# The last quarter of a down projection with tokens as rows, its earlier sum turned by VectorE

## The reference

```python
def conv_ffn(x, prev, up, cw, cb, down):
    a = x @ up
    gate, val = jnp.split(a, 2, axis=-1)
    gc, new = causal_conv(gate, prev, cw)
    h = jax.nn.gelu(gc + cb, approximate=True) * val
    return h @ down, new
...
    f, new_ffn = conv_ffn(rmsnorm(x, g_ffn_pre), ffn_prev, ffn_up, ffn_conv_w, ffn_conv_b, ffn_down)
    x = x + rmsnorm(f, g_ffn_post)
```

## Time and profile before

| | |
|---|---|
| median of three runs | 1332.47 us (1332.05 to 1333.07) |
| the profiled execution: its own time | 1332.47 us |
| the profiled execution: span from first to last instruction | 1330.8 us |
| mean granted TensorE clock | 0.999 |
| busy share of the span: PE, PEld, DVE, ACT, POOL | 99%, 99%, 60%, 38%, 5% |
| mean DMA rate | 150 GB/s |

### The profile page before, as it was taken

One profiled execution on the slowest core, in us unless ns is written; L12 is line 12 of the kernel. 1 busy time (PEld: TensorE's weight loads), 2 busy tenths in 40 slices (PEclk: granted clock), 3 DMA queues, 4 the chain that ended last, 5 costly groups with the idle time before them and its releaser, 6 DMA issues.

```text
span 1330.8 us, 24552 instructions
## 1 busy us (share of the span) xinstructions
PE 1319.8 (99%) x8970; PEld 1312.0 (99%) x8970; DVE 798.7 (60%) x1256; ACT 500.6 (38%) x726; POOL 73.2 (5%) x186
## 2 busy tenths in 40 slices
PE   9999999999999999999999999999999999999997
PEld 8999999999999999999999999999999999999996
DVE  7758755544488655556655544555555455655875
ACT  7323333234464333323333332333333333333552
POOL 0051000000041000000000000000000000000000
PEclk9999999999999999999999999999999999999999
DMA  9754455565554554556455455645544565555453
GB/s 245 199 158 128 133 147 138 157 160 139 155 134 134 152 157 128 140 148 183 133 152 156 131 137 152 180 138 153 150 137 131 152 180 145 151 146 138 131 145 129
DMA packets 378792, 199.61 MB, mean 150 GB/s; under 512 B 4216, under 2 KB 375588, under 8 KB 378748
## 3 DMA queue, kind: packets, MB, share of 16 engines
q1 hardware_dynamic: 377940, 198.16, 54.2%
q10 hardware_dynamic: 736, 0.66, 0.2%
q0 software_dynamic: 80, 0.31, 0.1%
HBM read 195.68 MB, written 3.56 MB: 150 GB/s over the span
## 4 chain that ended last, share of the span: by engine, by line
PE 98%; DVE 1%; DMA 0%; issue 0%; SPq 0%; ACT 0%; DVEq 0%; ACTq 0%
PE mm L552 31%; PE mm L556 31%; PE mm L553 31%; DVE y_rows L1807 1%; PE tb L811 1%; PE tb L552 1%; PE tb L815 1%; PE tb L556 1%; PE tb L812 1%; PE tb L553 1%; PE tb L642 0%; DMA x_tok<-in_x_sample_dram 0%; PE tb L856 0%; PE tb L731 0%; PE mm L900 0%; PE mm L901 0%
## 5 line engine op out<-in xcount | busy, mean ns | idle before, releaser
L552 PE MATMUL mm<-a_hi,w_hi 128*128 128x320 f32 x1856 | 577.1, 311 | 0.2
L556 PE MATMUL mm<-a_lo,w_hi 128*128 128x320 f32 x1856 | 573.6, 309 | 0.0
L553 PE MATMUL mm<-a_hi,w_lo 128*128 128x320 f32 x1856 | 573.6, 309 | 0.0
L960 ACT ACTIVATE w_hi<-raw 128x1024 fp32r (+3 forms) x378 | 346.8, 965 | 441.7 <-PE mm L556 431.4
L1289 DVE TENSOR_TENSOR w_lo<-raw,w_hi 128x1024 fp32r<-128x1024 f32 (+1 forms) x376 | 409.5, 1130 | 112.9 <-ACT w_hi L960 112.2
L552 PEld LDWEIGHTS mm<-a_hi,w_hi 128*128 128x128 f32 x1856 | 348.5, 188 | 1.6 <-DVE w_lo L1330 0.5
L553 PEld LDWEIGHTS mm<-a_hi,w_lo 128*128 128x128 f32 x1856 | 348.5, 188 | 0.3
L556 PEld LDWEIGHTS mm<-a_lo,w_hi 128*128 128x128 f32 x1856 | 348.4, 188 | 0.0
L556 PE MATMUL mm<-m_lo,w_hi 128*128 128x320 f32 x884 | 273.2, 309 | 0.0
L552 PE MATMUL mm<-h_hi,w_hi 128*128 128x320 f32 x660 | 204.6, 310 | 0.0
L553 PE MATMUL mm<-h_hi,w_lo 128*128 128x320 f32 x660 | 204.0, 309 | 0.0
(11 more groups left out here) (277 smaller groups left out, 938.0 us busy)
## 6 DMA issues: line engine op xcount, KB each, us to landing
raw<-in_ffn_up_dram SPq DMA_DIRECT2D x88, 1024.0 KB, 5.8
raw<-in_ffn_down_dram SPq DMA_DIRECT2D x60, 704.0 KB, 4.8
raw<-in_w_in_dram SPq DMA_DIRECT2D x31, 1024.0 KB, 5.7
raw<-in_w_out_dram SPq DMA_DIRECT2D x16, 1024.0 KB, 6.0
raw<-in_ffn_down_dram SPq DMA_DIRECT2D x2, 1024.0 KB, 5.1
raw<-in_w_in_dram SPq DMA_DIRECT2D x3, 512.0 KB, 10.5
out_dram<-y_rows SPq DMA_DIRECT2D x6, 256.0 KB
x_tok<-in_x_prompt_dram SPq DMA_DIRECT2D x5, 256.0 KB, 4.3
```

The costliest lines, as they stand in the source:

```text
L552: pe.matmul(out, whi[:, s], hi, start=start, stop=False)
L553: pe.matmul(out, wlo[:, s], hi, start=False, stop=False)
L556: return pe.matmul(out, whi[:, s], tile(lo, k), start=False, stop=stop)
L960: act.activation(w_hi[:, d:d + half], src, ACT.Copy).then_inc(w_hi_done, 1)
```

## The change

The down projection of the last group is made wholly with tokens as rows: four blocks of 512 columns, each in the three PIECES, so 12 steps s = 0 to 11 in place of 12 chunks and three pieces. In each step of the first three blocks the order is tile 0, tile 1, tile 2; in the last block it is as before (tiles 2 and 0 through all three pieces, then tile 1). There are four sets of banks (`ROW_BANKS`), and `BANK_FREE` says which step waits for which bank. The first three blocks start in empty banks, and VectorE adds the sum of the first three groups afterwards (`add_rows`). That sum, 12 blocks of `f`, is turned by VectorE in blocks of 32x32 (`turn_f`): for tiles 0 and 1 it is written to the six `tb` banks during the last group's up steps, three instructions after each step, and ScalarE copies the six banks to `f_tok` when the up projection is over; for the samples eight instructions write to SBUF (`f_s`). ScalarE squares rows and sums them along the row (`square_block`), VectorE multiplies by the gain (`gain_block`), which is now loaded as a whole (128x2048) to the place of `f`. The transposes of `turn_unit` for f, `token_sums(4)`, the addition of blocks, their squares and their sum in `acc` are gone. The transposes of the states (seven), of the last block's earlier sum (eight, `seed_rows`) and of the samples' (four) stay.

```diff
+        ROW_BANKS = [(mm[0], mm[1], tb[0]), (tb[3], tb[1], tb[4]), (tb[2], tb[5], mm[0]), (mm[1], tb[3], tb[0])]
+        F_BANKS = [(b, i) for b in range(QD - 1) for i in range(2)]
...
+                if s == 4:
+                    sp.wait_ge(f_blocks, N_F_BLOCKS + 8)
+                    sp.dma_start(gain[:, :], g_ffn_post.to_broadcast([P, D])).then_inc(gain_b_in, 16)
...
+            BANK_FREE = {(0, 0): (drained[0], c_rows // 2), (0, 1): (drained[1], c_rows // 2),
+                         (0, 2): (taken, len(F_BANKS)), (2, 0): (taken, len(F_BANKS) + 2), (2, 2): (rows_added, 1),
+                         (3, 2): (rows_added, 3)}
+            for s in range(3 * QD - 3):
+                b, j = s // 3, s % 3
+                pe.wait_ge(w_lo_done, 2 * (c_rows + s) + 2)
+                if b == 0:
+                    pe.wait_ge(h_hi_done, h0 + sum(PIECES[j]))
+                    pe.wait_ge(h_lo_done, h0 + sum(PIECES[j]))
+                for i in range(3):
+                    if j == 0 and (b, i) in BANK_FREE:
+                        pe.wait_ge(*BANK_FREE[b, i])
+                    last = rows(i, s)
+                    if i == 2:
+                        last.then_inc(used, 1)
+                    elif j == 2:
+                        last.then_inc(rows_done, 1)
+                    if i == 0:
+                        if s in (4, 5):
+                            turn_ffn_states(s - 4)
+                        if s == 7:
+                            turn_samples()
+                        if s == 8:
+                            seed_rows(0)
+                            seed_rows(1)
+            pe.wait_ge(*BANK_FREE[3, 2])
+            for s in range(3 * QD - 3, 3 * QD):
+                pe.wait_ge(w_lo_done, 2 * (c_rows + s) + 2)
+                last = rows(2, s)
...
                 act.preload_act_table(ACT.Sqrt)
-                for m in range(WIDE):
...
+                act.wait_ge(f_blocks, N_F_BLOCKS)
+                act.wait_ge(used, c_rows)
+                for b, i in F_BANKS:
+                    act.activation(f_tok[3 * b + i][:, :], tb[3 * i + b][:, :], ACT.Copy).then_inc(taken, 1)
+                act.wait_ge(ssq_zeroed, 1)
+                for s in range(1, 3 * QD - 2):
+                    split_wide(s + 1)
+                    if s == 3 * QD - 3:
+                        split_wide(s + 2)
+                    if s in (4, 5):
+                        take_states(s - 4)
+                    if s % 3 == 0:
+                        copy_lows(s // 3 - 1)
+                        square_block(s // 3 - 1)
...
+            def turn_f(i, b, a):
+
+                t0 = TT[i][0] + 32 * b
+                dst = f_s[32 * b:32 * b + 32, :] if i == 2 else \
+                    tbs[32 * b:32 * b + 32, (QD - 1) * 512 * i:(QD - 1) * 512 * (i + 1)]
+                dve.transpose(dst.rearrange("p (k c) -> p k c", c=P)[:, :, 32 * a:32 * a + 32],
+                              f[32 * a:32 * a + 32, 0:WIDE * T].rearrange("p (k t) -> p k t", t=T)[:, :, t0:t0 + 32]
+                              ).then_inc(f_blocks, 1)
+
+            def last_up_steps():
+                g = GROUPS - 1
+                f_todo = [(i, b, a) for i in range(2) for b in range(4) for a in range(4)]
+                for i in range(NG):
+                    up_step(g, i, g * NG + i,
+                            blocks=[4 * nk for _, nk in PIECES[0:2]] if i == NG - 1 else (KD, KD))
+                    for block in f_todo[3 * i:3 * i + 3]:
+                        turn_f(*block)
...
+                dve.wait_ge(used, c_rows)
+                for b in range(2):
+                    for a in range(4):
+                        turn_f(2, b, a)
+                dve.wait_ge(f_blocks, N_F_BLOCKS + 8)
+                dve.wait_ge(taken, len(F_BANKS))
+                for s in range(1, 3 * QD - 1):
+                    if s < 3 * QD - 2:
+                        split_wide(s + 1)
+                    if s == 3 * QD - 3:
+                        split_wide(s + 2)
+                    if s % 3 == 0:
+                        add_rows(s // 3 - 1)
+                    if s == 4:
+                        dve.wait_ge(gain_b_in, 16)
+                    if s % 3 == 1 and s > 3:
+                        gain_block(s // 3 - 1)
+                    for block in BLOCKS[EARLY_BLOCKS + PER_CHUNK * (s - 1):EARLY_BLOCKS + PER_CHUNK * s]:
+                        turn_block(*block)
```

More of the change, by code:

```diff
@@ L176, in hybrid_layer @@
     assert at["ws"] + D * 4 <= at["conv_hist"]
[L177 to L188, removed]
+    c_rows = 2 * (C_FFN // 2 + (GROUPS - 1) * (PER_GROUP // 2) + NG)
+    f_s = sb("f_s", [P, (QD - 1) * 512], where="a_hi", plus=28672)
+    f_tok = [f_s[:, n // 3 * 512:(n // 3 + 1) * 512] if n % 3 == 2 else
+             sb(f"f_tok{n}", [P, 512], where="a_hi", plus=16384 + 2048 * (n // 3 * 2 + n % 3))
+             for n in range(3 * (QD - 1))]
+    f_tok += [sb("f_last0", [P, 512], where="a_hi", plus=34816),
+              sb("f_last1", [P, 512], where="a_hi", plus=36864),
+              sb("f_last2", [P, 512], where="f", plus=D * 4 + 2048)]
+    junk = sb("junk", [P, 512], where="a_hi", plus=38912)
+    gain = sb("gain", [P, D], where="f")
+    s_low = sb("s_low", [TS, 512], where="f", plus=D * 4)
+    ssq = sb("ssq", [P, 3 * QD], where="conv_hist")
+    rest = sb("rest", [P, 4], where="conv_hist", plus=64)
+    most = sb("most", [P, 4], where="conv_hist", plus=96)
     wx_hi = sb("wx_hi", [P, 4 * 512], F32R, where="xT")
@@ L495, in load_group @@
                     load(q, 1, wcols(up, NF + g * NG + i))
[L496 to L501, removed]
+                if n_pairs:
+                    with sp.Fori(0, n_pairs) as i:
+                        q = C_FFN // 2 + g * (PER_GROUP // 2) + NG + i
+                        for e in range(2):
+                            rows = down[:, g * NG:(g + 1) * NG] if type(g) is int else \
+                                down[:, bass.ds(g * NG, NG)]
+                            load(q, e, rows[:, :, bass.ds((2 * i + e) * P, P)], NG)
             load_group(0, KD // 2, 3)
@@ L925, in _ @@
-                if j == 1:
-                    pe.wait_ge(drained[1], q_end)
-                    token_sums(4)
-            for j in range(len(PIECES)):
-                last = rows(1, j)
+            for s in range(3 * QD - 3, 3 * QD):
+                last = rows(1, s)
             last.then_inc(rows_done, 1)
@@ L1156, in up_step @@
                 if not early:
[L1157 removed]
+                    split_hi(q + 1, 1, blocks[1])
             def up_steps(g, i0=0):
@@ L1161, in up_steps @@
                     up_step(g, i, g * NG + i)
-                up_step(g, NG - 1, g * NG + NG - 1, blocks=NG)
+                up_step(g, NG - 1, g * NG + NG - 1,
+                        blocks=[4 * nk for _, nk in PIECES[0:2]] if type(g) is int and g == GROUPS - 1 else (NG, NG))
             def group(g, last):
```

257 lines of the change are left out of this document (112 added, 145 removed).

## The result

The changed kernel takes 1335.99 us in the median (1333.84 to 1337.58, 13 executions), the kernel before in the same comparison 1332.57 us (1332.03 to 1333.99, 13 executions): a ratio of 1.0021, with a 95% interval of 1.0013 to 1.0028. It is slower by about 0.2%, 2.2 us over the 1333.8 that was predicted and 0.2 us inside the upper end of the range. That it lies inside the range is luck: the range reached up there for late weights, which did not come, and was meant to leave out the clock, whose own range began at 1335.5 us. The scatter is the first thing to notice: 3.7 us between executions, where before had 2.0.

A forecast was written before the change was run, and what follows sets the result against it. TensorE, busy 99% of the span, was taken to bound the kernel. A saving of 2.28 us, a 3.1 us wait and 0.47 us of VectorE lateness gave +1.3 on 1332.47: 1333.8 us, range 1330.5 to 1336.2.

The forecast's parts named there:

- late weights: Slower rival in the last group's steps: VectorE's splits or a load come late; two us of waits give 1335.8; chance 0.12.
- the clock: Slower rival at the seam: TensorE's clock falls to half in the gap, giving 1335.5 to 1340.6 us; chance 0.08.
- TensorE's work: Last group, until the samples are done: 72.37 us in place of 74.65, a saving of 2.28 us (1.51 to 2.89).
- The seam: After the up projection, tile 2 of step 0 waits for ScalarE's six copies: TensorE stands still 3.1 us (2.8 to 3.6).
- The steps: Down projection steps of 7.3 or 5.5 us run without a wait for weights; closest is step 2, 2 us to spare.
- the third rival: Weights late, slower: additions, gains and turns delay VectorE's splits, or the 1 MB gain holds up a load; chance 0.12.
- The end: Ahead of `f_last`, VectorE's splits, additions, gains and small sums make it 0.47 us late (0 to 1.1).
- The sum: Whole kernel: -2.28 + 3.1 + 0.47 = +1.3, giving 1333.8 us, bounds 1332.4 to 1335.3; chance 0.62.
- the row: Clock windows at the run's end: granted clock falls to half 4.6 us after TensorE's end, so 3.1 us pass unpunished.
- the prediction's own signs of being wrong: VectorE's PSUM writes far over 0.7 us, the clock row leaving 1.00 behind the seam, or weights waited for.

The follow-up runs named there:

- c: The change with tile 0's three banks copied first, each tile's copies waiting only for its own 16 turns, tile 2 for its own bank's copy: 1330.30 us, ratio 0.9984.
- b: The change, but tile 2 of step 0 waits only for the copy freeing its own bank, block 1's tile 0 for the sixth: 1330.96 us, ratio 0.9986.
- f_best: c with the samples' third of the last gain moved on VectorE behind the second half of `f_last`: 1329.91 us, ratio 0.9984 to the kernel before.
- d_filled: The change with thirteen products with zeros as weights ahead of the seam's wait, so TensorE works through the hole: 1333.32 us, ratio 1.0005.
- a_same: The changed kernel again, nothing edited, for a second profiled execution: 1334.67 us, ratio 1.0016 to the kernel before.
- e: The change with three more ScalarE copies into an unread buffer ahead of the six, for a longer hole: 1337.10 us, ratio 1.0037.
- h: The same kernel as c, unchanged, run again beside f_best on the same chip: 1330.09 us, ratio 0.9984 to the kernel before.

## Why the prediction was right in its sum and missed the median

- **TensorE's work**: predicted 72.37 us, measured 72.63 (run c). With the 2.07 for the transposes that is 0.2298 for each of the 307 products in place of 0.229; the saving is 2.02, not 2.28. Right within its bounds.
- **The seam**: predicted 3.1 us, the row says 3.15, and it costs 75.74 (1313.73 - 1237.99) - 72.63 = 3.11. The steps were right too: VectorE ends `m_lo` 2.38 us after the seam (2.37), splits for 1.83 (1.82), turns twice in 1.23 (1.14: a turn to PSUM is 0.62 there, between the bounds), and ScalarE copies for 3.04 (3.0). That it is this wait, and not the turns themselves, that costs is shown by b and c: with it shorter or gone the change gains 0.14 to 0.16%.
- **The steps**: no wait of TensorE for weights in any profile. Right, and with it the third rival falls.
- **The end**: predicted 0.47 us of lateness. `f_last` starts 1.05 us after the samples are done, 0.98 before, and 0.90 in f_best, where nothing stands ahead of it: VectorE is 0.15 late, which puts +0.07 in the sum. Right in kind and too large, since the three gains were done (1314.28) when the copy of `s_low` ended (1314.53), and only the small sums were not.
- **The sum**: -2.02 + 3.11 + 0.07 = +1.16 (predicted +1.3). d_filled, which has the hole's length and no fall, takes 1333.32 us, and the point was 1333.8; over the kernel before on its own chip that is +0.6 in the median (-0.5 to +1.9), so the medians hold less of the +1.16 than the traces, and why is not known. The upper bound of the sum was added up wrongly: -1.51 + 3.6 + 1.1 gives 1335.7, not 1335.3. And a difference under 0.2% can be told from none here: the 0.14% of b has an interval that ends below 1 (0.9977 to 0.9995).
- **The clock**: this is the step that failed. I wrote "By this row 3.1 us pass unpunished", and gave the rival 0.08. The row shows one execution in which the clock fell 4.6 us after the last product. That says that it can stay up so long, not that it must: in a_same it fell 2.3 us and in e 2.0 us after the last product. The end of the run, where that row was read, shows it too: in the thirteen profiles the clock falls there between 1.95 us (b, rows below) and 4.7 us after the last product, and the kernel before has the longest of them. A clock row that leaves 1.00 behind the seam was one of the prediction's own signs of being wrong, and it came. The size of the fall was inside the rival's bounds: 14 products and 2.8 us, between its 8 products (1.7) and 32 (6.8), and the 1336.1 us of the execution in which the fall is seen stand in its 1335.5 to 1340.6. The rule of the Trainium skill that was set against the row, "TensorE: Matmul & The Clock Gate", section "Why this matters for your kernels", no gaps over about 3 us, was the better guide: a_same loses the clock at 3.15. It isn't a sharp limit, though: the first profiled execution kept full clock at 3.15, and at 2.17 seven of eleven executions show a lower mean clock, with medians to match.

The end of b, where the last product is over at 1320.46 + 0.39 = 1320.85 and the clock falls at 1322.8 (columns as above):

```profile
1322.00:1323.00 1.00, 0.00 (x0) 0.00 (x0) 0.86 (x6) 0.00 (x0) 0.00 (x0) 0.90 1.08 318
1323.00:1324.00 1.00, 0.00 (x0) 0.00 (x0) 1.00 (x3) 0.00 (x0) 0.00 (x0) 0.50 1.01 322
```

Take the kernel without a hole (1330.2, the mean of c and h) and add the hole (the runs are from several chips, on which the kernel before differs by up to 0.6 us): 1330.9 at 0.70, 1331.9 at 1.7, 1332.4 at 2.17, 1333.35 at 3.15, 1335.2 at 5.03. The medians lie on this line at 0.70 (1330.96) and 1.7 (1331.76), and at 3.15 where the hole is filled (1333.32). They lie over it by 1.6 at 2.17, by 1.3 and 2.6 at 3.15 and by 1.9 at 5.03. At 3.15 and 5.03, where the rows show the fall and what it costs (2.8 and 1.8), that is the clock's part; at 2.17 it is argued. Open is why the 13 executions of the first comparison had more of it than the 11 of the second, and how much of a mean of 0.997 is the fall at the seam: four of 33 executions of the kernel before, which has no hole, have 0.997 too. The mean also holds the half clock at the end of the span, 3.7 to 6.4 us long in the thirteen profiles, which by itself makes it 0.998 or 0.999; so 0.997 says that there was more half clock, but not where.

## What to carry to other kernels

A new wait on TensorE has two prices, its length and what the clock takes behind it, and the second can come and go between executions: when the scatter grows with a change, compare the mean clocks of the executions before believing the one that was profiled, and take a second profile to see where the clock fell. One stretch that passed at full clock sets no floor for the next; test the doubt by filling the hole with work that does nothing, which took 1.35 us off here. Better still is to have no hole: each bank waits only for its own copy, and what is needed first is copied first, which made a change that cost 0.2% into one that gains 0.16%.

## What was not expected of the hardware

The granted clock was half for the same time in both profiled falls, about 1245.0 to 1251.9 and 1244.7 to 1251.5, though TensorE stood still for 3.15 us in one and 5.03 in the other. So the longer hole lost fewer products to the clock (8 against 14); two executions are too few for a rule. VectorE's turns to PSUM and to SBUF cost nearly the same, as the groups by shape of the changed kernel show (xcount | busy us, mean ns | idle before us):

```profile
L1718 DVE STREAM_TRANSPOSE tb<-f 32x384 f32<-32x384 f32 x32 | 18.9, 589 | 1.0
L1718 DVE STREAM_TRANSPOSE f_s<-f 32x384 f32<-32x384 f32 x8 | 4.5, 568 | 0.2
```
